# Retention heads: output by token instead of by feature, norm from per-row statistics, a turned head, and the context's score first

## The reference, cut to what matters

```
scores = einsum(q_chunk, k_chunk) * decay          # per head, both directions
y      = scores @ v + (q * xi) @ state             # 256 features per token and head
mu     = mean(y, over the 256 features)
var    = mean((y - mu)^2)
yn     = (y - mu) * rsqrt(var + 1e-6)
y_ret  = silu(gate) * (yn * gn_gain)               # then y_ret @ w_ret_out
state' = (k * zeta)^T @ v                          # context only, an output
```

## Time and profile before

| | us |
|---|---|
| median of 3 runs | 2425.44 (2423.05 to 2428.73) |
| the profiled execution | 2423.81 |
| its span | 2422.0 |
| TensorE busy in it | 2302.2 (95%) |
| VectorE busy | 1304.5 (54%) |
| ScalarE busy | 852.5 (35%) |

### The profile page before, as it was taken

How to read it: one execution, slowest core, us unless ns; L and a number is a source line. 1 busy time by engine, 2 the same in 40 slices (tenths; PEclk the granted TensorE clock), 3 DMA queues, 4 the chain that set the end, 5 groups by cost and what they waited for, 6 DMA issues and landing times.

```text
span 2422.0 us, 33466 instructions
## 1 busy us (share of the span) xinstructions
PE 2302.2 (95%) x14296; PEld 2139.9 (88%) x14296; DVE 1304.5 (54%) x1875; ACT 852.5 (35%) x1347; POOL 85.9 (4%) x161
## 2 busy tenths in 40 slices
PE   7999989999998999999989999999999999999997
PEld 2999989988987898998979999999989799999996
DVE  2555567566665767676565555424654444343444
ACT  3454432255334212112255444324553332121212
POOL 0000001000000000000000000000000000000000
PEclk8999999999999999999999999999999999999999
DMA  6111145322443444343413111222222321222121
GB/s 254 57 61 62 61 135 175 109 82 70 158 104 122 154 136 137 122 145 107 95 29 109 62 62 57 70 90 89 80 83 79 121 88 62 88 70 79 61 88 44
DMA packets 59748, 233.58 MB, mean 96 GB/s; under 512 B 7313, under 2 KB 7345, under 8 KB 57425
## 3 DMA queue, kind: packets, MB, share of 16 engines
q1 hardware_dynamic: 41040, 153.12, 19.6%
q0 software_dynamic: 18560, 78.33, 9.4%
HBM read 223.00 MB, written 8.42 MB: 96 GB/s over the span
## 4 chain that ended last, share of the span: by engine, by line
PE 75%; DVE 13%; ACT 6%; issue 3%; DMA 1%; DVEq 1%; ACTq 0%; POOL 0%; SPq 0%; POOLq 0%
PE unit L394 15%; PE unit L395 15%; PE unit L397 15%; PE unit L382 9%; PE unit L384 8%; PE unit L383 8%; DVE junk L1359 3%; DVE wl L1260 2%; ACT wh L930 1%; PE sc L382 1%; DVE rs L1393 1%; PE unit L475 1%; PE unit L511 1%; PE sc L384 1%; PE sc L383 1%
## 5 line engine op out<-in xcount | busy, mean ns | idle before, releaser
L394 PE MATMUL unit<-hmh,wh 128*128 128x320 f32 x2304 | 697.5, 310 | 13.7 <-DVE vl L1270 10.4
L395 PE MATMUL unit<-hml,wh 128*128 128x320 f32 x2304 | 694.9, 310 | 0.0
L1260 DVE TENSOR_TENSOR wl<-raw,wh 128x1024 fp32r<-128x1024 f32 x276 | 335.3, 1222 | 452.3 <-ACT wh L930 446.2
L397 PE MATMUL unit<-hmh,wl 128*128 128x320 f32 x2304 | 525.6, 309 | 0.0
L394 PEld LDWEIGHTS unit<-hmh,wh 128*128 128x128 f32 x2304 | 433.3, 188 | 18.5 <-issue 16.6
L395 PEld LDWEIGHTS unit<-hml,wh 128*128 128x128 f32 x2304 | 433.3, 188 | 2.0
L397 PEld LDWEIGHTS unit<-hmh,wl 128*128 128x128 f32 x2304 | 385.8, 188 | 0.0
L930 ACT ACTIVATE wh<-raw 128x1024 fp32r<-128x1024 f32 x276 | 283.5, 1048 | 114.6 <-DMA raw<-w_main 114.5
L1359 DVE CUSTOM_DVE_ANT_0 junk<-ada,csb,par 128x1024 f32<-128x1024 f32 x160 | 205.5, 1285 | 24.5 <-DMA ada<-w_ada 4.4
L382 PE MATMUL unit<-wh,hmh 128*128 128x256 f32 (+1 forms) x640 | 203.1, 317 | 9.3 <-DVE t L1286 6.1
L384 PE MATMUL unit<-wh,hml 128*128 128x256 f32 (+1 forms) x640 | 200.6, 313 | 0.0
(11 more groups left out here) (279 smaller groups left out, 3436.5 us busy)
## 6 DMA issues: line engine op xcount, KB each, us to landing
raw<-w_main SPq DMA_DIRECT2D x276, 512.0 KB, 3.7
ada<-w_ada POOLq DMA_DIRECT2D x80, 512.0 KB, 3.9
bias<-biases POOLq DMA_DIRECT2D x16, 640.0 KB, 5.3
first<-w_first SPq DMA_DIRECT2D x8, 1024.0 KB, 21.2
x<-x POOLq DMA_DIRECT2D x2, 2560.0 KB, 12.2
gains<-g_rows POOLq DMA_DIRECT2D x4, 1024.0 KB, 5.0
x_keep<-x POOLq DMA_DIRECT2D x1, 2560.0 KB, 8.9
x<-x_keep POOLq DMA_DIRECT2D x1, 2560.0 KB, 10.7
```

The source lines that it names most:

```text
L394: pe.matmul(u[:, h, 0:n], a[0], xs[h][0], start=f, stop=False)
L395: pe.matmul(u[:, h, 0:n], a[0], xs[h][1], start=False, stop=False)
L397: mm = pe.matmul(u[:, h, 0:n], a[1], xs[h][0], start=False, stop=z)
L1260: dve.tensor_tensor(wl[slot[i]][:, :], raw[slot[i]][:, :], f32(wh[slot[i]][:, :]), ALU.subtract)\
```

## The change

The output of a head is computed with tokens on the partitions: the weighed scores are the stationary side and the values the moving side, 256 columns at a time; first the context's tile into one unit, then the four latent tiles into the other. The context's state is computed before them. Mean and variance are then per partition: VectorE's `bn_stats` and `bn_aggr` give them for each of five token tiles, ScalarE takes five roots, VectorE five reciprocals and five (y - mean) x 1/root. TensorE turns the normalised head back with ten 128x128 transposes, the latent ones into a unit, the context's into `sc[0]`, and VectorE multiplies by gain and gate straight from there. The scores are computed in the order 4, 0, 1, 2, 3 (4 is the context's). The matrix of ones and its fill go.

```diff
+ORDER = (4, 0, 1, 2, 3)
-        ones = fixed("ones", [P, P])
-        y = r1("y", [P, 2, T])
+        y = r1("y", [P, TILES, DV])
...
-                def feature_sums(of):
-
+                def turn_head():
+
+                    pe.wait_ge(yn_scaled, heads.count)
+                    pe.wait_ge(p_full, heads.count * 5)
                     u = U.take()
-                    for hf in range(2):
+                    for t in range(TILES):
                         for c in range(2):
+                            out = u[:, c, t * P:(t + 1) * P] if t < 4 else sc[0][:, c * P:(c + 1) * P]
+                            mm = pe.transpose(out, y[:, t, c * P:(c + 1) * P], ident[:, :])
                     U.give(mm)
...
                     else:
                         column()
-                        head_means()
                         column()
-                        head_squares()
+                        turn_head()
                     values()
...
+                    def score(n):
+                        i = ORDER[n]
+                        if n == 0:
+                            pe.wait_ge(yret_ready, heads.count)
...
-                    for c in range(2):
-                        u = U.take()
-                        cols = slice(c * P, (c + 1) * P)
-                        for i in range(4):
-                            if c == 0:
-                                pe.wait_ge(p_ready, heads.count * 5 + i + 1)
-                            product(u[:, 0, :], (vh[:, i, cols], vl[:, i, cols]),
-                                    (ph[:, i * NS:(i + 1) * NS], pl[:, i * NS:(i + 1) * NS]), i == 0, False)
...
                     mm.then_inc(st_psum, 1)
 
+                    u = U.take()
+                    pe.wait_ge(p_ready, heads.count * 5 + 1)
+                    U.give(product(u[:, 0, 0:DV], (ph[:, 4 * NS:], pl[:, 4 * NS:]), (vh[:, 4, :], vl[:, 4, :]), True, True))
+                    u = U.take()
+                    pe.wait_ge(s0_ready, heads.count + 1)
+                    pe.wait_ge(qd_ready, heads.count + 1)
+                    for t in range(4):
+                        out = u[:, t // 2, t % 2 * DV:(t % 2 + 1) * DV]
+                        for i in range(4):
+                            if t == 0:
+                                pe.wait_ge(p_ready, heads.count * 5 + i + 2)
+                            at_ = slice(i * NS + t * P, i * NS + (t + 1) * P)
+                            product(out, (ph[:, at_], pl[:, at_]), (vh[:, i, :], vl[:, i, :]), i == 0, False)
+                        for d in range(2):
+                            at_ = slice(t * P, (t + 1) * P)
+                            mm = product(out, (qdh[:, d, at_], qdl[:, d, at_]), (s0h[:, d, :], s0l[:, d, :]), False, d == 1)
+                    U.give(mm)
...
-            def head_deviations():
-
-                U.add()
-                U.wait_released(1)
-                act.activation(sq2[:, :, :], y[:, :, :], ACT.Square).then_inc(ysq_ready, 1)
...
             def head_root():
+                act.wait_ge(yv_ready, heads.count)
+                act.activation(y_sd[:, :], y_mv[:, :, 1], ACT.Sqrt, bias=epsc[:, 0:1]).then_inc(ysd_ready, 1)
...
+                    u = U.get()
+                    U.release(act.activation(y[:, 4, :], u[:, 0, 0:DV], ACT.Copy))
+                    u = U.get()
+                    U.release(act.activation(y[:, 0:4, :], u[:, :, :].rearrange("p a (b n) -> p (a b) n", b=2), ACT.Copy))
...
+            def head_stats():
+                U.wait_released(3)
+                U.wait_released(2)
+                for t in range(TILES):
+                    dve.bn_stats(y_stats[:, t, :], y[:, t, :])
+                dve.drain()
+                for t in range(TILES):
+                    a = dve.bn_aggr(y_mv[:, t, :], y_stats[:, t, :])
+                a.then_inc(yv_ready, 1)
+
+            def head_scaled():
+                dve.wait_ge(ysd_ready, heads.count)
+                dve.reciprocal(y_rs[:, :], y_sd[:, :])
+                dve.drain()
+                for t in range(TILES):
+                    a = dve.tensor_scalar(y[:, t, :], y[:, t, :], y_mv[:, t, 0:1], y_rs[:, t:t + 1], ALU.subtract, ALU.mult)
+                a.then_inc(yn_scaled, 1)
...
             def head_norm(h):
                 u = U.get()
...
                 for c in range(2):
+                    a = dve.scalar_tensor_tensor(out=yret[:, h * 2 + c, 0:NS], in0=u[:, c, :], scalar=gain[c],
+                                                 in1=sg[:, c, 0:NS], op0=ALU.mult, op1=ALU.mult)
+                U.release(a)
+                for c in range(2):
+                    a = dve.scalar_tensor_tensor(out=yret[:, h * 2 + c, NS:T], in0=sc[0][:, c * P:(c + 1) * P], scalar=gain[c],
+                                                 in1=sg[:, c, NS:T], op0=ALU.mult, op1=ALU.mult)
...
                         U.add()
                         split()
                         if h and n == 0:
-                            head_means()
+                            head_stats()
+                        elif h:
+                            head_norm(h - 1)
...
+                        if h and n == 0:
+                            head_scaled()
...
-                    if h:
-                        head_norm(h - 1)
                     wait_hi()
...
                         if j == 0 and c == 0:
-                            head_means()
+                            head_stats()
+                            head_scaled()
```

More of the change, by code:

```diff
@@ L538, in _ @@
                     pe.transpose(tp[0][:, 0:P], ks[:, NS:T], ident[:, :]).then_inc(kt_ready, 1)
[L540 to L543, removed]
+                    def score(n):
+                        i = ORDER[n]
+                        if n == 0:
+                            pe.wait_ge(yret_ready, heads.count)
+                        if n >= 2:
+                            pe.wait_ge(p_full, heads.count * 5 + n - 1)
+                        w = NS if i < 4 else P
                         keys = [t[:, i * P:(i + 1) * P] for t in (kh, kl)]
                         qrs = [t[:, 0:NS] if i < 4 else t[:, NS:T] for t in (qh, ql)]
-                        product(sc[i % 2][:, 0:n], keys, qrs, True, True).then_inc(sc_ready, 1)
+                        product(sc[n % 2][:, 0:w], keys, qrs, True, True).then_inc(sc_ready, 1)
                     score(0)
@@ L584, in _ @@
                     column()
-                    if j == 0:
-                        head_means()
                     column()
                     if j == 0:
-                        head_squares()
+                        turn_head()
                     column()
@@ L1036, in _, with p_split @@
                     act.activation(kzh[:, :, :], kz[:, :, :], ACT.Copy).then_inc(kz_hi, 1)
[L1038 to L1041, removed]
+                    def p_split(n):
+                        act.wait_ge(p_full, heads.count * 5 + n + 1)
+                        i = ORDER[n]
+                        w = NS if i < 4 else P
+                        act.activation(ph[:, i * NS:i * NS + w], pst[:, n % 2, 0:w], ACT.Copy).then_inc(p_hi, 1)
                     def gate_c(c):
@@ L1055, in _ @@
                     split()
[L1056 to L1061, removed]
                     act.wait_ge(st_psum, heads.count + 1)
@@ L1077, in _ @@
                         split()
-                        if j == 0 and c < 2:
-                            (head_deviations, head_root)[c]()
+                        if j == 0 and c == 0:
+                            head_root()
+                        elif j == 0 and c == 1:
+                            U.add()
                         if j == 0 and c == 1:
@@ L1380, in scales_ffn @@
                 dve.memset(flag[:, :], 0.0).then_inc(gm_ready, 1)
-            def head_means():
-                u = U.get()
[L1385 to L1396, removed]
+            def head_stats():
[7 more added lines that the diff above has]
+                a.then_inc(yv_ready, 1)
@@ L1397, in head_norm @@
+            def head_scaled():
[5 more added lines that the diff above has]
+                a.then_inc(yn_scaled, 1)
+            def head_norm(h):
+                u = U.get()
                 if h == 0 and layer.count:
                     dve.wait_ge(x_saved, layer.count * 16)
+                gain = [par[:, layer.count, GN + h * 2 + c:GN + h * 2 + c + 1] for c in range(2)]
@@ L1399, in head_norm @@
                 for c in range(2):
-                    a = dve.scalar_tensor_tensor(out=yret[:, h * 2 + c, :], in0=y[:, c, :],
-                                                 scalar=par[:, layer.count, GN + h * 2 + c:GN + h * 2 + c + 1],
-                                                 in1=sg[:, c, :], op0=ALU.mult, op1=ALU.mult)
+                    a = dve.scalar_tensor_tensor(out=yret[:, h * 2 + c, 0:NS], in0=u[:, c, :], scalar=gain[c],
+                                                 in1=sg[:, c, 0:NS], op0=ALU.mult, op1=ALU.mult)
```

58 lines of the change are left out of this document (19 added, 39 removed).

## The result

| | before | changed |
|---|---|---|
| median of 5 runs, us | 2425.44 (2422.98 to 2428.73) | 2410.96 (2404.53 to 2413.70) |
| ratio (95% interval) | | 0.9938 (0.9920 to 0.9956) |
| profiled execution, its span | 2423.81, 2422.0 | 2410.36, 2408.6 |
| TensorE's mean granted clock in it | 0.984 | 0.981 |

What follows compares the result with a forecast made beforehand. TensorE was taken as the bound; six heads at -2.0 us, two layer ends at -2.5 each and +0.6 for two more heads gave about -16.5 us, so 2408 us, range 2395 to 2422.

Steps and rivals of the forecast that it cites:

- What bounds it: TensorE, busy 95% of the span: a head's length is the sum of its matmuls plus one gap.
- Sums removed: On TensorE, `feature_sums` twice a head goes: 2.15 us per sum, 4.3 us per head, 34.4 us for 8 heads.
- Transposes: Ten added on TensorE in `turn_head`, 0.116 us each: 1.2 us per head, 9.3 in all.
- Products: On TensorE, values as moving side: 75 matmuls of 256 columns in 9.0 us, cost +0.15 per head, +1.2 in all.
- Rival 3: 33 more weight loads a head on TensorE show in the open, 6.2 us x 8 = 50: 2458; chance 0.02.
- The vl gap: TensorE's gate column no longer waits for VectorE's `vl`: the 1.7 us gap goes in 6 heads, -10.4 us.
- The new wait: TensorE waits at `turn_head` for VectorE's scaled output: 2.5 us in 6 heads, 0.6 us at two layer ends.
- The last tile: With the context's score first, TensorE waits for the last, 512-wide weighed tile: 0.15 us per head, 1.2 in all.
- Nothing given back elsewhere: VectorE and ScalarE bound no head, the layer-0 stage moves with TensorE, and weight slabs cost nothing.
- Rival 1: No new wait at the turn, statistics taking 1.6 us: about 2391 at best, 2400 halfway; chance 0.15.

Runs made afterwards that it cites:

- experiment 5: Kernel before, without the 128x640 reciprocal in head_norm (y multiplied by the root, not its inverse): 2418.05 us, ratio 0.9970 against the kernel before.
- experiment 2: Changed kernel with the statistics taken early, while VectorE waits for the decay's exponentials: 2392.66 us, ratio 0.9873 against the kernel before.
- experiment 3: Changed kernel with statistics early, plus root ahead of ScalarE's q copy and scaling ahead of VectorE's split: 2388.98 us, ratio 0.9858 against the kernel before.
- experiment 4: Changed kernel with the five bn_stats done two times: 2432.55 us, ratio 1.0035 against the kernel before.
- experiment 6: Kernel before, with each sum over features taken over the first 128 of 256 only: 2422.63 us, ratio 0.9992 against the kernel before.

## Why the prediction was right, point by point

The direction and the size were right. By its own steps:

- **What bounds it.** TensorE's sum plus one gap. Right.
- **Sums removed, 4.3 us per head.** Right: L511 is gone, and with the other terms as measured a head comes out: -4.3 + 1.15 - 1.96 + 2.1 + 0.2 + 0.2 = -2.6.
- **Transposes, 0.116 each.** Right: from 133.81 to the first matmul of `values` (135.08 less one spacing of 0.12) is 1.15 us for ten. The 275 ns that the Trainium skill gives for one ("TensorE: Matmul & The Clock Gate", Part 4: PE-mode transpose) are again the duration of one, 273 ns in this trace, and not its price in a row of ten.
- **Products, 9.0 us for 75.** Right: 108.35 to 117.63, the 75 and their 0.2 wait, is 9.28. Rival 3 is out: each of these loads 128 columns anew and they start 0.12 apart. The rule in the Trainium skill ("TensorE: Matmul & The Clock Gate", Part 3, "What overlaps and what doesn't"), by which a load overlaps running matmuls only in another row group, does not hold for these.
- **The vl gap, -10.4.** Right, and larger: the list of waits counts from the end of the last matmul, and by the distance of starts the gap is worth 1.96 a head (experiment 5), 11.8 in all.
- **The new wait, 2.5 us in heads and 0.6 at layer ends.** The mechanism, the place and the releaser are right; the list has 1.95 and 0.47, just under the "2 to 3" that the prediction gave for the heads. By the distance of starts, as the prediction reckoned it, it is 2.1 and 0.6. `bn_stats` is 0.33 apart as taken, `bn_aggr` 0.07 instead of 0.1 with less for the drain (2.16 us in all, 2.4 forecast), rotation and scaling are 0.15 shorter: 0.4 a head, 2.4 us over six.
- **The last tile, 0.15.** 0.2 measured.
- **Nothing given back elsewhere.** Wrong: the forecast has the clock nowhere. It read 1.00 in the head of the earlier trace rows and took it for the changed kernel's too. But the change moved a wait of TensorE to another place, and there it brings stretches at half clock: three and four of them in the two profiles, 5 and 7 us of lost time, beside the 7.6 that the changed kernel loses more in the mean of its runs.

So the sum was too small by 5 us at full clock: -21.6 and not -16.5. The gap (1.4), the wait (2.4) and the products and the last tile (0.8 the other way) explain 3 of these, and 2 are not placed. The missing clock term has the opposite sign, so that 2408 met 2411 better than the sum deserved: that closeness is luck.

Rival 1 (no new wait, 2391) is what experiments 2 and 3 make of the kernel, at 2393 and 2389: its price was right, its condition wrong for this order of the code.

## What to carry to other kernels

When a wait on the bounding engine is removed, look at once at what the engine meets next, and count the clock with it: here each us of waiting at the turn cost 1.4 to 1.5 us by the medians (17.8 us for 12.6 of waits in experiment 2, 22 for 14.5 in experiment 4). Work that needs nothing but a finished buffer belongs at a point where its engine is idle, not behind an operation that waits for something newer; five statistics moved by some ten lines were worth more than the change itself. Span times mean granted clock compares kernels to 1 or 2 us where the times scatter by several, and distances of starts from head to head in two traces agree to 0.02 us. When a profiled execution is the fastest of its set, as in experiments 5 and 6, it doesn't show what the others lost.

## What the runs showed of the hardware

- TensorE's granted clock: 1.95 us without matmuls, followed by ten fp32 transposes (1.15 us), brought a stretch at the lower level in 7 of 12 cases, beginning 0.1 to 1.4 us behind the first transpose; 1.7 us among matmuls in 0 of 12, 2.75 us among matmuls in 2 of 6; 2.3 us of transposes without a wait in 0 of 8. A stretch made a head of 59.0 us 1.5 to 1.6 longer (60.50 to 60.62).
- `bn_stats` over 128x256 fp32 takes 0.41 us and the next starts 0.33 later; `bn_aggr` over the six values of a row 0.15 and 0.07. A reciprocal over 640 columns takes 4.14 us, over 5 columns 0.18.
- A whole program's loss to the clock differs between executions of one kernel by some 10 us: spans of the kernel before lie between 2418.4 at 0.986 and 2429.5 at 0.981.
